# Last projection units reordered, layer norm and pooling moved between units, and the gate row summed in the middle of the kernel

## The chip, the cores and the metric

One core of a Trainium2 chip. The core has five engines that each run their own list of instructions in order: TensorE (PE in the rows; PEld is its weight load), VectorE (DVE), ScalarE (ACT), GpSimd (POOL) and SyncE (SP, which issues most transfers; GpSimd issues the rest). They meet only through semaphores: an instruction waits until a counter has reached a value. The metric is the device time of one execution in microseconds (us).

## What is computed

One mixer layer for 2,048 latent positions of width 1,024 and 256 context positions, in float32:

```python
hx = rmsnorm(x, g_pre) * (1 + sc_x) + sh_x              # sc, sh, gt = silu(c) @ w_mod + b_mod
ux = hx @ w_in                                          # 1024 -> 2304 = 18 tiles of 128
vx_lru, gx_lru, vx_pool, gx_pool, vx_conf, ggx_conf, gx_conf = split(ux)
y_lru  = bidirectional RG-LRU(dwconv4(vx_lru))          # gates by matmul, two scans, context first
y_pool = (window means - v) @ pool_w * pool_scale
y_conf = silu(layernorm(dwconv31(vx_conf * sigmoid(ggx_conf)))) @ conf_pw
z = concat(y_lru * silu(gx_lru), y_pool * silu(gx_pool), y_conf * silu(gx_conf))
out = x + gt_x * rmsnorm(z @ w_out, g_post)             # gt_x: the gate row, 1024 numbers
```

## The kernel before

Every float32 product of weight and activation is three matmuls on a high and a low half (`mm3`: hi·hi, hi·lo, lo·hi), so each operand is first split: ScalarE or GpSimd rounds the high half, VectorE or GpSimd subtracts it.

**Units.** The normalised, transposed input lies in `xTh` and `xTl` (8 blocks of 128 rows by 2,048 positions). A projection unit (o, c) computes tile o of the 18 for chunk c of 512 positions: 24 matmuls of 512 columns into one of two PSUM banks. ScalarE copies the bank into one of two slots of `ustage` (`evac`), and SP stores the slot to DRAM (`store_u`). `evac(U)` waits until the store of unit U-2 has landed; unit U waits until U-2 is evacuated. Sixteen further units (`conv`, 15 matmuls of 256 columns) are the 31-tap convolution. `UNITS` is the list of all 88, numbered 0 to 87 here; tiles are taken in the order `ORDER`, and each tile's weights are loaded into the slot of the tile two before it (`load_w`, `w_hi`, `w_lo`).

**Steps.** Beside the units runs the LRU in 20 steps q (4 channel tiles by 5 pieces). `gates(q)` are 12 matmuls that TensorE runs right behind unit `GATES_AFTER[q]`. Then ScalarE does `sigmoids(q)` and `decays(q)`, one `evac`, `roots(q)` (a square root on what VectorE's `one_minus_a2` left), and the other evacuations up to unit `GATES_AFTER[q+1]`, which come ahead of `sigmoids(q+1)` in its list. VectorE ends the step with `scans(q)`. The units behind `GATES_AFTER[5]` to `[12]` are 19, 22, 26, 29, 32, 37, 40, 43.

**SP's list.** For each unit in order: `store_u(n)`, then `after_unit(n)`, which issues what hangs on that unit: the next tile's weights and the inputs and weights of a later convolution.

**Tail.** `TAIL` is a list of tokens that every engine walks, each doing its own part of a token: `unit`; for chunk c of the layer norm `mu` (mean), `var`, `swish`, `pw` (pointwise product); for half-chunks n of the pooling `pool` (sums) and `pmm` (product); `wo` k (load and split of W_out block k); `item` n (one block of z: load y and gate, silu, multiply, split); and before also `gate` and `gmm` (gate row by 16 matmuls). Of the 20 units behind the last gates, 14 run first; the last 6 have `mu` to `pmm` of chunks 0 and 1 between them; chunks 2 and 3 follow with `wo` and `item` behind them. W_out and z lie where `xTh` and `xTl` were, so their loads begin when the last unit is done:

```python
if kind == "gate":
    sp.wait_ge(s_pu, N_CU + len(UNITS))
```

GpSimd walks the tail only behind this, which produces what the first `mu` needs (`onesk`, `la`):

```python
pool.wait_ge(s_ys, 64 * N_LRU)
pool.wait_ge(s_pu, N_CU + CONV_AT[-1] + 1)
g.memset(pwr[:], 0.0).then_inc(s_twz, 1)
g.memset(onesk[:], 1.0 / 256.0).then_inc(s_twz, 1)
```

**Stage 5.** 16 output tiles of 128 positions, 48 matmuls each; the z items of the next chunk are made meanwhile, three ahead.

Of the kernel before, what the change touches and what calls it, by code (L numbers as in the profile page):

```python
# [91 lines left out]
def mixer_kernel(nc, x, ctx, par, w_mod, b_gate, g_post, w_in, gate_w, pool_w, conv_dw, conf_pw, w_out,  # L92
# [6 lines left out]
    with es:  # L99
# [93 lines left out]
        crep = a4.take("crep", [P, KD, P])  # L193

        a5 = Area(x0, w0)
        woh = a5.take("woh", [P, KD, D], f32r)
        wol = a5.take("wol", [P, KD, D], f32r)
        z1 = a5.off
        zh = a5.take("zh", [P, 2, KD, CH], f32r)
        zl = a5.take("zl", [P, 2, KD, CH], f32r)  # L200

        zsize = 4 * KD * CH
        wg = [at("wg0", [P, KD, CH], z1 + zsize), at("wg1", [P, KD, CH], z1 + 3 * zsize)]
        ab = Area(w0, r0)
        wor = ab.take("wor", [P, 2, D])
        yb = ab.take("yb", [P, 3, CH])
        gb = ab.take("gb", [P, 3, CH])
# [153 lines left out]
        for c in range(NCH + 1):
            now, before = c < NCH, c > 0
            steps = [("mu", c) if now else None, ("swish", c - 1) if before else None,
                     ("pmm", 2 * c - 1) if before else None, rest.pop(0) if rest and now else None,
                     ("pool", 2 * c) if now else None,
                     rest.pop(0) if rest and now else None, ("var", c) if now else None, ("pw", c - 1) if before else None,
                     ("pool", 2 * c + 1) if now else None, ("pmm", 2 * c) if now else None,
                     rest.pop(0) if rest and now else None]
            for token in [token for token in steps if token]:
                TAIL.append(token)  # L370
                if ("unit", len(UNITS) - 1) in TAIL and token[0] in SIDE_BEHIND:
                    TAIL += side[:SIDE_PIECES]
                    side = side[SIDE_PIECES:]
# [12 lines left out]
        def _(sp):  # L386
# [96 lines left out]
            def load_item(n):  # L483

                c, k = ITEMS[n]
                if n >= 3:
                    sp.wait_ge(s_zl, n - 2)
                if c == 0 and k == 4:
                    sp.wait_ge(s_pys, 32)
                if c == 0 and k == 6:  # L490
                    sp.wait_ge(s_lys, 32)
# [1 line left out]
                gt = (G_LRU + k) if k < 4 else (G_POOL + k - 4) if k < 6 else (G_CONF + k - 6)
# [2 lines left out]
            def load_wg(h):
                for m in range(2):
                    sp.dma_start(wg[h][:, :, m * 256:(m + 1) * 256], w_mod[8 + 2 * h + m]).then_inc(s_wg[h], 16)

            def load_wo(k):  # L500
                if k >= 2:
                    sp.wait_ge(s_wol, k - 1)
                sp.dma_start(wor[:, k % 2, :], w_out[k * P:(k + 1) * P, :]).then_inc(s_wor[k % 2], 16)

            for kind, n in TAIL:
                if kind == "gate":
                    sp.wait_ge(s_pu, N_CU + len(UNITS))
                    sp.wait_ge(s_wlo, len(W_JOBS))
                    sp.wait_ge(s_ys, 64 * N_LRU)
                    for b in range(2):  # L510
                        sp.wait_ge(s_us[b], 16 * (N_CU + len(UNITS)) // 2)
                    load_wo(0)
                    load_item(0)
                    load_wo(1)
                    load_item(1)
                    load_item(2)
                    load_wg(0)
                if kind == "wo" and n + 2 < KD:
                    load_wo(n + 2)
# [2 lines left out]
                if kind == "item" and n == 0:
                    load_wg(1)
# [1143 lines left out]
```

## Time and profile before

| | us |
|---|---|
| median of 3 runs | 914.27 (913.06 to 915.58) |
| the profiled execution | 916.63 |
| its span, first to last instruction | 914.8 |
| TensorE busy | 788.8 |
| VectorE, ScalarE, GpSimd busy | 485.4, 455.2, 394.0 |
| mean granted TensorE clock | 0.943 |

TensorE is busy for 86% of the span. A busy TensorE is at one of two clocks, 2.4 GHz (granted clock 1.0) or 1.2 GHz, and the clock of a stretch is the mean. The idle time ahead of an instruction says more than the share: who ended it stands in brackets in the timeline.

### The profile page before, as it was taken

What the parts mean: (1) busy time and instruction counts of PE and PEld (TensorE: products, weight loads), DVE (VectorE), ACT (ScalarE), POOL (GpSimd) and SP (SyncE); (2) the same over time, 40 slices, a digit from 0 to 9 for tenths busy, and PEclk for the clock granted to TensorE, in tenths of its full rate; (3) what the DMA queues carried; (4) which work ended last, traced back from release to release, by engine and by line L of the source; (5) the groups of instructions that cost most, each with busy time, mean ns of one, the idle gap of its engine ahead of it and who ended that gap; (6) DMA issues with size and microseconds to landing.
All of it is one profiled execution on the core that took longest, in us unless ns stands there. A gap on an engine that the chain in (4) does not pass through costs nothing.

```text
span 914.8 us, 9881 instructions
## 1 busy us (share of the span) xinstructions
PE 788.8 (86%) x3496; PEld 622.0 (68%) x3496; DVE 485.4 (53%) x653; ACT 455.2 (50%) x749; POOL 394.0 (43%) x405
## 2 busy tenths in 40 slices
PE   6687998999879899899889969999547399999996
PEld 2266786888767687778677758867324287878785
DVE  4388834538744875547543300054657557475732
ACT  4265634797558856768657601114345134344311
POOL 0278444566537646555654441113303135252521
PEclk9797998999999999999999979999878799999998
DMA  9992013235332443333321332223895176657532
GB/s 366 345 275 110 35 58 104 72 86 162 109 85 73 134 146 108 103 124 109 109 84 47 115 95 70 70 92 110 237 321 157 51 276 207 219 196 233 182 116 101
DMA packets 84914, 130.10 MB, mean 142 GB/s; under 512 B 22689, under 2 KB 49953, under 8 KB 83329
## 3 DMA queue, kind: packets, MB, share of 16 engines
q1 hardware_dynamic: 80496, 115.44, 38.8%
q0 software_dynamic: 4368, 14.03, 5.6%
q8 instruction: 28, 0.46, 0.2%
q14 instruction: 22, 0.17, 0.1%
HBM read 91.17 MB, written 38.27 MB: 141 GB/s over the span
## 4 chain that ended last, share of the span: by engine, by line
PE 47%; issue 14%; ACT 13%; DVE 11%; POOL 8%; DMA 4%; SPq 3%; POOLq 0%; ACTq 0%; DVEq 0%
PE bank L1419 14%; PE bank L1421 14%; PE bank L1420 14%; SPq L392 2%; DVE zl L1365 2%; PE bank L1561 2%; ACT L928 2%; ACT Qb L929 2%; ACT Ib L916 1%; ACT bank L930 1%; DMA wraw<-in_w_in 1%; POOL zh L564 1%; DVE yb L1363 1%; DVE xTl L1157 1%; POOL Ib L658 1%
## 5 line engine op out<-in xcount | busy, mean ns | idle before, releaser
L1419 PE MATMUL bank<-xTh,wh 128*128 128x512 f32 (+1 forms) x592 | 238.2, 402 | 41.6 <-ACT ustage L903 10.6
L1421 PE MATMUL bank<-xTh,wl 128*128 128x512 f32 (+1 forms) x592 | 234.7, 396 | 0.0
L1420 PE MATMUL bank<-xTl,wh 128*128 128x512 f32 x576 | 230.4, 400 | 0.0
L1419 PEld LDWEIGHTS bank<-xTh,wh 128*128 128x128 f32 x592 | 114.9, 194 | 69.9 <-issue 35.6
L1421 PEld LDWEIGHTS bank<-xTh,wl 128*128 128x128 f32 x592 | 114.6, 194 | 24.3
L1420 PEld LDWEIGHTS bank<-xTl,wh 128*128 128x128 f32 x576 | 112.4, 195 | 23.5 <-issue 0.2
L1419 PE MATMUL bank<-woh,zh 128*128 128x512 f32 x256 | 100.0, 391 | 4.0 <-DVE zl L1365 3.2
L903 ACT ACTIVATE ustage<-bank 128x512 f32<-128x512 f32 x56 | 33.5, 600 | 135.2 <-PE bank L1421 135.1
L1420 PE MATMUL bank<-wol,zh 128*128 128x512 f32 x256 | 99.6, 389 | 0.0
L1421 PE MATMUL bank<-woh,zl 128*128 128x512 f32 x256 | 99.6, 389 | 0.0
L1086 ACT ACTIVATE sqj<-bank 128x512 f32<-128x512 f32 x32 | 18.8, 595 | 108.6 <-PE bank L1421 108.6
L687 POOL TENSOR_TENSOR wl<-wraw,wh 128x1024 fp32r<-128x1024 f32 x16 | 38.8, 2423 | 67.5 <-ACT wh L853 67.5
L564 POOL TENSOR_SCALAR sph<-xc 128x512 fp32r<-128x512 f32 (+1 forms) x36 | 23.2, 660 | 99.4 <-DVE xc L1106 51.1
L564 POOL TENSOR_SCALAR zh<-yb 128x512 fp32r<-128x512 f32 x32 | 19.9, 620 | 107.2 <-DVE yb L1363 107.2
L1419 PEld LDWEIGHTS bank<-woh,zh 128*128 128x128 f32 x256 | 48.0, 188 | 15.6 <-DVE zl L1365 4.4
L1106 DVE SCALAR_TENSOR_TENSOR bank<-Qb,bank 128x512 f32<-128x512 f32 (+1 forms) x40 | 25.4, 641 | 57.0 <-ACT bank L930 57.0
L1421 PEld LDWEIGHTS bank<-woh,zl 128*128 128x128 f32 x256 | 48.0, 188 | 10.0
L1420 PEld LDWEIGHTS bank<-wol,zh 128*128 128x128 f32 x256 | 48.1, 188 | 9.8
L1106 DVE SCALAR_TENSOR_TENSOR xc<-vbuf,prm,xc 128x512 f32<-128x512 f32 (+1 forms) x60 | 52.0, 866 | 2.1
L658 POOL TENSOR_TENSOR Ib<-Ib,xc 128x512 f32<-128x512 f32 (+1 forms) x40 | 46.9, 1194 | 1.1 <-ACT Ib L916 1.0
L564 POOL TENSOR_SCALAR xTh<-fbuf 128x512 fp32r<-128x512 f32 (+1 forms) x40 | 33.9, 867 | 31.0 <-ACT fbuf L887 30.8
L853 ACT ACTIVATE wh<-wraw 128x1024 fp32r<-128x1024 f32 x18 | 19.2, 1066 | 53.3 <-DMA wraw<-in_w_in 53.3
(190 smaller groups left out, 1536.8 us busy)
## 6 DMA issues: line engine op xcount, KB each, us to landing
scratch_u<-ustage SPq DMA_DIRECT2D x72, 256.0 KB, 2.5
wraw<-in_w_in SPq DMA_DIRECT2D x18, 512.0 KB, 4.1
wm<-in_w_mod SPq DMA_DIRECT2D x8, 1024.0 KB, 11.2
xg<-in_x SPq DMA_DIRECT2D x16, 512.0 KB, 8.8
yb<-scratch_y SPq DMA_DIRECT2D x32, 256.0 KB, 3.1
gb<-scratch_u SPq DMA_DIRECT2D x32, 256.0 KB, 4.7
xres<-in_x SPq DMA_DIRECT2D x16, 512.0 KB, 4.7
out<-tout SPq DMA_DIRECT2D x16, 512.0 KB, 2.9
```

The costliest lines, as they stand in the source:

```text
L392: sp.dma_start(rows(g, i, 0, KD), src[i * P:(i + 1) * P, :].rearrange("p (k j) -> p k j", j=P)).then_inc(s_xin[g], 16)
L564: return g.tensor_scalar(dst, src, 1.0, 1.0, ALU.mult, ALU.mult)
L658: g.tensor_tensor(out=I, in0=I, in1=xc_piece(c), op=ALU.mult).then_inc(s_ix, 1)
L687: g.tensor_tensor(out=l, in0=w_raw(w), in1=h.bitcast(f32), op=ALU.subtract).then_inc(s_wlo, 1)
L853: a.activation(W_JOBS[w][1][0], w_raw(w), ACT.Copy).then_inc(s_whi, 1)
L903: ins = a.activation(ustage[:, U % 2, :], pu[U % 2][:], ACT.Copy)
L928: a.activation(Ab[:, d, 0:n], r, ACT.Exp, scale=kn[:, kc:kc + 1]).then_inc(s_aq, 1)
L1086: a.activation(sqj[:, h * CH:(h + 1) * CH], ob[m % 3][h][:], ACT.Square, accum_out=ss2[:, h:h + 1]).then_inc(s_osq, 1)
L1106: return v.scalar_tensor_tensor(out=out, in0=in0, scalar=sc, in1=in1, op0=op0, op1=op1)
L1419: mm(out, wh_, xh_, start=first, stop=False)
L1420: mm(out, wh_, xl_, start=False, stop=False)
L1421: return mm(out, wl_, xh_, start=False, stop=last)
```

## The change

Three things are done together.

1. The last eight projections are taken in another order, so that chunks 0 and 1 of `xTh`/`xTl` are read for the last time four units before the end. W_out goes into these columns (raw and low half in the same place), z into chunks 2 and 3.
2. All of the layer norm and pooling is woven between the first 14 of the 20 units behind the last gates. Six units follow with `wo` 0 to 7 and `item` 0 to 7 behind four of them.
3. The gate row is no longer made by 16 matmuls on 4 MB of weights loaded in the tail. It is made in eight pieces of 128 columns during steps 5 to 12: SP loads piece m into `wgp` (one buffer), VectorE sums it over k in 8 instructions behind `scans(5 + m)`, and two matmuls with `onesk` behind the first output tile add up the partitions.

The first output tile also waits per block k, with both halves of the output inside the loop over k.

```diff
+PROJECTIONS = [(o, c) for c in range(NCH) for o in (0, 1)] + [(o, c) for o in range(2, NT_IN - 2) for c in range(NCH)]
+PROJECTIONS += [(16, 0), (16, 1), (17, 0), (17, 1), (16, 2), (17, 2), (16, 3), (17, 3)]
...
+GATE_STEP = [5 + m for m in range(8)]
+GATE_PIECE_AT = [GATES_AFTER[q - 1] for q in GATE_STEP]
...
-        TAIL, rest = rest[:-6], rest[-6:]
...
+        TAIL = []
         for c in range(NCH + 1):
+            now, after = c < NCH, c > 0
+            TAIL += [("mu", c)] if now else []
+            TAIL += [("swish", c - 1), ("pmm", 2 * c - 1)] if after else []
+            TAIL.append(rest.pop(0))
+            TAIL += [("pool", 2 * c)] if now else []
+            TAIL.append(rest.pop(0))
+            TAIL += [("var", c)] if now else []
+            TAIL += [("pw", c - 1)] if after else []
+            TAIL += [("pool", 2 * c + 1), ("pmm", 2 * c), rest.pop(0)] if now else []
+        HALF_DONE, THREE_DONE = PROJ_AT[-5], PROJ_AT[-3]
+        side = [("wo", k) for k in range(KD)] + [("item", k) for k in range(KD)]
+        while rest:
+            TAIL.append(rest.pop(0))
+            behind = 0 if TAIL[-1][1] < HALF_DONE else 4 if TAIL[-1][1] < THREE_DONE else 3
+            TAIL += side[:behind]
+            side = side[behind:]
         TAIL += side
...
                     if n == LAST_OF[o - 2]:
                         load_w(o + 2)
+                for m in range(KD):
+                    if n == GATE_PIECE_AT[m]:
+                        if m:
+                            sp.wait_ge(s_ga, m)
+                        sp.dma_start(wgp[:], w_mod[8 + m // 2, :, :, m % 2 * P:m % 2 * P + P]).then_inc(s_wg, 16)
...
             def load_wo(k):
-                if k >= 2:
-                    sp.wait_ge(s_wol, k - 1)
-                sp.dma_start(wor[:, k % 2, :], w_out[k * P:(k + 1) * P, :]).then_inc(s_wor[k % 2], 16)
+                if k == 0:
+                    sp.wait_ge(s_pu, N_CU + HALF_DONE + 1)
+                sp.dma_start(wo_raw(k), w_out[k * P:(k + 1) * P, :]).then_inc(s_wor[k], 16)
...
                 if kind == "unit":
                     store_u(N_CU + n)
                     after_unit(n)
+                    if n == HALF_DONE:
+                        for k in range(KD):
+                            load_wo(k)
+                        for k in range(3):
+                            load_item(k)
...
+            def gate_sum(m):
+
+                dve.wait_ge(s_wg, 16 * (m + 1))
+                acc = gacc[:, m * P:(m + 1) * P]
+                link(v.tensor_scalar(acc, wgp[:, 0, :], cs[:, 0:1], None, ALU.mult))
+                for k in range(1, KD - 1):
+                    link(stt(acc, wgp[:, k, :], cs[:, 2 * k:2 * k + 1], acc, ALU.mult, ALU.add))
+                k = KD - 1
+                stt(acc, wgp[:, k, :], cs[:, 2 * k:2 * k + 1], acc, ALU.mult, ALU.add).then_inc(s_ga, 1)
...
                 scans(q)
+                if q in GATE_STEP:
+                    gate_sum(GATE_STEP.index(q))
...
+            def gate_row():
+
+                pe.wait_ge(s_ga, KD)
+                pe.wait_ge(s_ev, N_CU + len(UNITS))
+                for h in range(2):
+                    mm(gob[h][:], onesk[:], gacc[:, h * CH:(h + 1) * CH], start=True, stop=True).then_inc(s_gmm, 1)
```

SP's list of transfers around step 5, before: the weights of a tile (`wraw`) behind unit 19, then the stores of units 20 (`scratch_u`) and 21 (`scratch_cv`, a convolution).

```order
43 L404 DMA wraw<-in_w_in 128x1024 [waits unit_done,w_lo]
44 L442 DMA scratch_u<-ustage 1024x1x64 [waits unit_evacuated]
45 L442 DMA scratch_cv<-ustage 128x256 [waits unit_evacuated]
46 L448 DMA cvwraw<-in_conv_dw 128x640 [waits unit_done]
47 L462 DMA cvz<-scratch_u 128x256 [waits u_stored0,u_stored1,unit_done]
```

The same place in the changed kernel; `gate_summed` is `s_ga`.

```order
44 L409 DMA wraw<-in_w_in 128x1024 [waits unit_done,w_lo]
45 L478 DMA wgp<-in_w_mod 128x8x128 [waits gate_summed]
46 L447 DMA scratch_u<-ustage 1024x1x64 [waits unit_evacuated]
47 L447 DMA scratch_cv<-ustage 128x256 [waits unit_evacuated]
48 L453 DMA cvwraw<-in_conv_dw 128x640 [waits unit_done]
49 L467 DMA cvz<-scratch_u 128x256 [waits u_stored0,u_stored1,unit_done]
```

The piece of gate weights, with its wait, stands between unit 19's weights and unit 20's store.

VectorE's list at the end of step 5 in the changed kernel, from the second scan on:

```order
140 L1252 SCALAR_TENSOR_TENSOR Qb<-Ab,Ib 128x256
141 L1259 COPY sml<-Qb 128x1
142 L1280 TENSOR_SCALAR gacc<-wgp,sml 128x128
143 L1105 SCALAR_TENSOR_TENSOR gacc<-wgp,sml,gacc 128x128 x7
144 L1221 TENSOR_SCALAR xc<-vbuf,prm 128x512
```

The eight instructions of the sum stand between the scan's last copy and the next piece's depthwise convolution (`xc`); before, 144 followed 141. What `gate_summed` counts is the last of them.

TensorE's list behind the last gates, before:

```order
1921 L1420 MATMUL bank<-spl,gwh 128x512
1922 L1421 MATMUL bank<-sph,gwl 128x512
1923 L1419 MATMUL bank<-xTh,wh 128x512 [waits unit_evacuated,hT_lo,w_lo]
1924 L1420 MATMUL bank<-xTl,wh 128x512
1925 L1421 MATMUL bank<-xTh,wl 128x512
```

and in the changed kernel:

```order
1921 L1426 MATMUL bank<-spl,gwh 128x512
1922 L1427 MATMUL bank<-sph,gwl 128x512
1923 L1535 MATMUL bank<-la,onesk 128x512 [waits scan_done,ln_in,tailw_zero]
1924 L1535 MATMUL bank<-la,onesk 128x512
1925 L1425 MATMUL bank<-xTh,wh 128x512 [waits unit_evacuated,hT_lo,w_lo]
```

`mu` 0 (`la`, `onesk`) now stands ahead of the units of tile 13, where it stood 14 units later.

## Rows read from the trace of the kernel before

**Rows 1.** The page: TensorE's busy time and share; GB/s moved in 40 slices.

```profile
PE 788.8 (86%) x3496; PEld 622.0 (68%) x3496; DVE 485.4 (53%) x653; ACT 455.2 (50%) x749; POOL 394.0 (43%) x405
...
GB/s 366 345 275 110 35 58 104 72 86 162 109 85 73 134 146 108 103 124 109 109 84 47 115 95 70 70 92 110 237 321 157 51 276 207 219 196 233 182 116 101
```

**Rows 2.** Busy time by stretch: length; PE, PEld, DVE, ACT, POOL; clock, DMA share, GB/s.

```profile
593.30:643.40 50.10, 46.34 (x182) 35.06 (x182) 26.04 (x34) 14.66 (x21) 10.49 (x15) 0.97 0.31 95
643.40:728.60 85.20, 43.07 (x99) 23.10 (x98) 54.30 (x68) 34.14 (x45) 21.02 (x31) 0.76 0.62 198
728.60:739.50 10.90, 10.89 (x48) 9.05 (x49) 2.58 (x4) 0.00 (x0) 0.00 (x0) 1.00 0.80 277
739.50:914.80 175.30, 164.34 (x722) 134.76 (x720) 98.66 (x129) 63.32 (x123) 59.13 (x56) 0.99 0.56 185
```

**Rows 3.** Timeline, TensorE: start, length, what, and in brackets idle time before and releaser.

```profile
506.24 0.40 PE L1421 MATMUL bank<-sph,gwl 128*128 128x512 f32 x1
...
535.99 0.80 PE L1419 MATMUL bank<-xTh,wh 128*128 128x512 f32 x1 [6.89 <-POOL wl L687]
...
593.12 0.59 PE L1529 MATMUL bank<-la,onesk 128*128 128x512 f32 x1
...
619.29 0.47 PE L1419 MATMUL bank<-pdh,pwh 128*128 128x512 f32 x1 [3.76 <-DVE pdl L1333]
...
645.85 0.47 PE L1419 MATMUL bank<-pdh,pwh 128*128 128x512 f32 x1 [0.76 <-issue]
```

**Rows 4.** Timeline, ScalarE, steps 5 to 12 (L901 evac, L853 w_hi, L912 sigmoids, L938 roots).

```profile
243.71 0.60 ACT L901 ACTIVATE ustage<-bank 128x512 f32<-128x512 f32 x1 [2.60 <-PE bank L1421]
...
265.63 0.60 ACT L901 ACTIVATE ustage<-bank 128x512 f32<-128x512 f32 x1 [4.66 <-PE bank L1421]
271.09 1.06 ACT L853 ACTIVATE wh<-wraw 128x1024 fp32r<-128x1024 f32 x1 [4.86 <-DMA wraw<-in_w_in]
...
274.58 0.66 ACT L912 ACTIVATE bank<-bank,prm 128x512 f32<-128x512 f32 x1
...
291.20 1.24 ACT L912 ACTIVATE bank<-bank,prm 128x512 f32<-128x512 f32 x2 [0.87 <-PE bank L1421]
...
300.51 1.07 ACT L938 ACTIVATE bank<-bank 128x512 f32<-128x512 f32 x2
...
368.38 1.24 ACT L912 ACTIVATE bank<-bank,prm 128x512 f32<-128x512 f32 x2 [0.88 <-PE bank L1421]
```

**Rows 5.** Timeline, VectorE: the copy that ends scans(5), and that of scans(8).

```profile
251.02 0.15 DVE L1260 COPY sml<-Qb 128x1 f32<-128x1 f32 x1
...
305.39 0.15 DVE L1260 COPY sml<-Qb 128x1 f32<-128x1 f32 x1
```

**Rows 6.** Instructions by line and shape, VectorE: count, busy us, mean ns, idle before.

```profile
L1106 DVE SCALAR_TENSOR_TENSOR bank<-Qb,bank 128x512 f32<-128x512 f32 x32 | 22.2, 695 | 55.3 <-ACT bank L930 55.3
...
L1106 DVE SCALAR_TENSOR_TENSOR bank<-Qb,bank 128x256 f32<-128x256 f32 x8 | 3.1, 423 | 1.7 <-ACT bank L930 1.7
```

**Rows 7.** DMA issues: count, KB each, median us from issue to landing.

```profile
scratch_u<-ustage SPq DMA_DIRECT2D x72, 256.0 KB, 2.5
wraw<-in_w_in SPq DMA_DIRECT2D x18, 512.0 KB, 4.1
...
gb<-scratch_u SPq DMA_DIRECT2D x32, 256.0 KB, 4.7
...
la<-scratch_cv POOLq DMA_DIRECT2D x8, 256.0 KB, 4.6
```

**Rows 8.** Timeline, GpSimd, behind the last step.

```profile
522.01 1.12 POOL L670 DMA_DIRECT2D scratch_y<-yrow  x2 [0.30 <-POOL yrow L667]
...
531.11 1.85 POOL L767 DMA_DIRECT2D la<-scratch_cv  x2
```

**Rows 9.** Timeline, VectorE, stage 5: the last instruction of two z items that follow each other.

```profile
746.89 0.69 DVE L1365 TENSOR_TENSOR zl<-yb,zh 128x512 fp32r<-128x512 f32 x1 [0.74 <-POOL zh L564]
...
748.93 0.69 DVE L1365 TENSOR_TENSOR zl<-yb,zh 128x512 fp32r<-128x512 f32 x1 [0.74 <-POOL zh L564]
```

More of the change, by code:

```diff
@@ L130, in mixer_kernel @@
         sml = fixed.take("sml", [P, 128])
+        gacc = fixed.take("gacc", [P, D])
         r0 = fixed.off
@@ L169, in mixer_kernel @@
         czl = a3.take("cvzl", [P, Z_SLOTS, NPH + 2 * REACH], f32r)
+        wgp = a3.take("wgp", [P, KD, P])
         a4 = Area(r0, end)
@@ L192, in mixer_kernel, with wo_hi, wo_lo, wo_raw @@
         onesk = a4.take("onesk", [P, P])
[L193 to L207, printed above, removed]
+        yb = a4.take("yb", [P, 3, CH])
+        gb = a4.take("gb", [P, 3, CH])
+        HALF = SEQ // 2
+        def wo_hi(k):
+            return xTh[:, k, 0:HALF]
+        def wo_lo(k):
+            return xTl[:, k, 0:HALF]
+        def wo_raw(k):
+            return xg[:, k, 0:HALF]
+        def z_cols(c):
+            return slice(HALF + c % 2 * CH, HALF + c % 2 * CH + CH)
         a6 = Area(r0, end)
@@ L278, in mixer_kernel @@
         s_pmm, s_pye, s_pys = sem("pool_product"), sem("pool_y"), sem("pool_y_stored")
-        s_wor, s_woh, s_wol = [sem(f"wo_in{b}") for b in range(2)], sem("wo_hi"), sem("wo_lo")
-        s_cr, s_gmm, s_gbc, s_gpo = sem("c_repeated"), sem("gate_product"), sem("gate_row"), sem("gpost_in")
-        s_wg = [sem(f"wgate_in{h}") for h in range(2)]
+        s_wor, s_woh, s_wol = [sem(f"wo_in{k}") for k in range(KD)], sem("wo_hi"), sem("wo_lo")
+        s_gmm, s_gpo = sem("gate_product"), sem("gpost_in")
+        s_wg, s_ga = sem("wgate_in"), sem("gate_summed")
         s_yg = [sem(f"yg_in{b}") for b in range(3)]
@@ L356, in mixer_kernel @@
         rest = [("unit", n) for n in range(GATES_AFTER[-1] + 1, len(UNITS))]
-        TAIL, rest = rest[:-6], rest[-6:]
-        side = [("gate", 0)] + [(kind, k) for k in range(KD) for kind in ("wo", "item")]
-        side[9:9], side[14:14] = [("gmm", 0)], [("gmm", 1)]
+        TAIL = []
         for c in range(NCH + 1):
[L362 to L373, printed above, removed]
+            now, after = c < NCH, c > 0
[14 more added lines that the diff above has]
+            side = side[behind:]
         TAIL += side
-        assert not rest
         ITEMS = [(c, k) for c in range(NCH) for k in range(KD)]
@@ L485, in load_item @@
                 c, k = ITEMS[n]
+                gt = (G_LRU + k) if k < 4 else (G_POOL + k - 4) if k < 6 else (G_CONF + k - 6)
                 if n >= 3:
                     sp.wait_ge(s_zl, n - 2)
+                elif n == 0:
+                    sp.wait_ge(s_ys, 64 * N_LRU)
                 if c == 0 and k == 4:
[L489 removed]
+                    sp.wait_ge(s_pys, 32 * NCH)
                 if c == 0 and k == 6:
[L491 removed]
+                    sp.wait_ge(s_lys, 32 * NCH)
+                U = unit_of(gt, c)
+                sp.wait_ge(s_us[U % 2], 16 * (U // 2 + 1))
                 sp.dma_start(yb[:, n % 3, :], y_dram[k, :, c * CH:(c + 1) * CH]).then_inc(s_yg[n % 3], 16)
[L493 removed]
                 sp.dma_start(gb[:, n % 3, :], u_dram[gt, :, c * CH:(c + 1) * CH]).then_inc(s_yg[n % 3], 16)
[L496 to L498 removed]
             def load_wo(k):
[L501 to L503 removed]
+                if k == 0:
+                    sp.wait_ge(s_pu, N_CU + HALF_DONE + 1)
+                sp.dma_start(wo_raw(k), w_out[k * P:(k + 1) * P, :]).then_inc(s_wor[k], 16)
             for kind, n in TAIL:
[L506 to L519, printed above, removed]
                 if kind == "item" and n + 3 < KD:
                     load_item(n + 3)
[L522 to L523 removed]
                 if kind == "unit":
@@ L1354, in out_weights_lo @@
                 dve.wait_ge(s_woh, k + 1)
-                v.tensor_tensor(out=wol[:, k, :], in0=wor[:, k % 2, :], in1=woh[:, k, :].bitcast(f32),
-                                op=ALU.subtract).then_inc(s_wol, 1)
+                v.tensor_tensor(out=wo_lo(k), in0=wo_raw(k), in1=wo_hi(k).bitcast(f32), op=ALU.subtract).then_inc(s_wol, 1)
             def z_item(n):
@@ L1376, in _ @@
                     ln_lo(n)
-                if kind == "gate":
-                    for b in range(2):
-                        dve.wait_ge(s_us[b], 16 * (N_CU + len(UNITS)) // 2)
-                    v.tensor_copy(crep[:], cs[:, 0:16:2].unsqueeze(2).to_broadcast([P, KD, P])).then_inc(s_cr, 1)
                 if kind == "wo":
@@ L1390, in _ @@
                 hs = slice(h * CH, (h + 1) * CH)
-                link(v.tensor_tensor(out=gbc[:, hs], in0=gbc[:, hs], in1=gob[h][:], op=ALU.add))
+                link(stt(gbc[:, hs], gob[h][:], 256.0, gbc[:, hs], ALU.mult, ALU.add))
                 link(v.tensor_tensor(out=gbc[:, hs], in0=gbc[:, hs], in1=gpo[:, hs], op=ALU.mult))
```

45 lines of the change are left out of this document (19 added, 26 removed).

## The prediction

> **What bounds the kernel now.** I read the page first, then the busy time by stretch, then TensorE's timeline for the brackets with idle time, and last the lists of ScalarE, VectorE, GpSimd and the queues around the places that the diff touches. TensorE is busy 788.8 us of 914.8 [rows 1], so it is the engine to watch, and there are two places where it waits. The large one is the stretch from 643.4, when the last unit is done, to 728.6, when the first output tile starts: 85.2 us with 43.1 busy, at a mean granted clock of 0.76, nearer to 1.2 than to 2.4 GHz, behind 0.97 ahead of it [rows 2]. The small one is in the steps. There ScalarE's list sets the pace: in step 8 it goes from the sigmoids (291.20) to the last root (301.6), and VectorE's scans end at 305.54, 14.3 us behind the sigmoids [rows 4, 5]. TensorE fits its units in between, with short pauses.
>
> I call S(q) the start of sigmoids(q) on ScalarE and E(q) the end of scans(q) on VectorE. E(5) is 251.2 and S(12) is 368.4 [rows 4, 5].
>
> **The middle: the gate row in eight pieces.** The work is small. A scalar_tensor_tensor takes 695 ns for 512 columns and 423 for 256 [rows 6]; on that line 128 columns are 0.29 us, with 0.03 to the next linked one 0.32, so a piece costs VectorE 8 x 0.32 = 2.6 us. Bounds: 8 x 0.19 = 1.5 us, if only the copy of one column (0.15 us [rows 5]) and some link were paid, and 8 x 0.51 = 4.1, somewhat over the 256-column form.
>
> The wait is not small. SP reaches piece m (m from 1) right behind the store of unit GATES_AFTER[m+4], the unit ahead of gates(m+4), and waits there for gate_sum(m-1), which VectorE does at the end of that same step m+4. SP is one list in order. Queued behind the waiting instruction are the stores of the step's units, the convolution's weights and inputs, and the next tile's weights. Call the unit n. evac(n+1) and evac(n+2) need only stores up to n. evac(n+3) needs store n+1, which is behind the wait, and it stands ahead of sigmoids(q+1) in ScalarE's list. So in each of steps 5 to 11, S(q+1) cannot come before E(q), the sum, the piece's issue, the landing of store n+1, and evac(n+3). Before, nothing tied the two so: evac(22), which is unit n+3 of step 5, ran at 243.7 [rows 4], and E(5) is 251.2.
>
> From the end of the sum to the landing of store n+1: at least 0.4 + 0.3 + 2.5 = 3.2 us if the store does not feel the piece ahead of it. A 512 KB load lands in 4.1 and a 256 KB store in 2.5 [rows 7], so 256 KB more are 1.6 and the pair would land in 5.7, if all packets went in line. I take 5.0, nearer the second, since the 512 KB go out right ahead in the same queue. Then evac 0.6 and table load 1.3: 6.9 us to S(q+1). That holds for steps 5, 10 and 11. The others have more behind the wait:
> - step 6: unit 25 is the last of its tile, so the next weights are issued only after it. From evac(25) to S(7) were 9.0 us (265.63 to 274.58, of them 4.86 for the weights [rows 4]); 5.0 + 9.0 = 14.0.
> - step 7: the convolution's weights follow the store and are rounded ahead of evac(29): 5.0 + 1.6 + 0.7 + 0.6 + 1.3 = 9.2.
> - step 8: tile weights, seventh in the queue, issued 2.7 after release, landing in some 5.5 (4.1 alone), then the 3.5 us from 271.09 to 274.58 [rows 4]: 11.7.
> - step 9 has five units: as step 7 up to evac(35) (7.9), then unit 37 (24 matmuls, 5.5) and 1.9 to the sigmoids: 15.3.
>
> Together 3 x 6.9 + 14.0 + 9.2 + 11.7 + 15.3 = 70.9. Seven sums are 18.2. S to E of steps 6 to 11: 14.3 in step 8, a little more where a convolution weight is rounded or two inputs are split; 6 x 14.8 = 88.8. S(12) is then 251.2 + 70.9 + 18.2 + 88.8 = 429.1 instead of 368.4: **+61 us**. Nothing later makes it good, because the steps behind are paced by the same list. With the low ends (sum 1.5, landing 3.2, 14.3 for S to E) it is 61 - 8 - 13 - 3 = 37; with the high ends (4.1, 5.7, and 15.5) 61 + 11 + 5 + 4 = 81.
>
> What the Trainium skill says of this place, in sentences the sum does without. Its page "DMA: Bandwidth & Descriptors", section "Anatomy of one DMA — SWDGE (gpsimd) path", states that DMA engines do not wait on semaphores and that the wait happens on the issuing sequencer ahead of dispatch; by that rule everything behind the piece is held, and it speaks against this change. The trace of before has no wait in SP's list that long ahead of stores, so it can't show it. The same section fits a transfer as 2.0 us plus bytes over 436 GB/s; the piece and the store are 0.79 MB, an estimate of 3.8 us where I take 5.0 less the store's 0.3 of issue, and the middle would be some 53 us by it.
>
> **The tail.** What starts later: `mu` 0 now stands directly behind gates(19), which end at 506.6 [rows 3]. It needs `onesk` and `la`; GpSimd makes them only after the last scratch_y transfer of 522.01 has landed, and issues `la` at 531.11, two transfers [rows 8] of 4.6 us to landing [rows 7], the second some 1 us later: 536.7. Before, the four units of tile 13 ran in that time and TensorE waited only 6.89 us, to 535.99 [rows 3]. Now all 30.1 us are idle. Then:
> - chunk 0, from `mu` 0 (593.1) to the product `pmm` 1 (619.3): 26.0 with its 3.76 us wait, and 2.4 for the first matmuls behind the pause at 1.2 GHz (12 at twice their time; behind the 6.89 us pause the first took 0.80 instead of 0.4 [rows 3]): 28.4.
> - chunks 1 to 3, each with three units: before, chunk 1 took 645.85 - 619.29 = 26.6 [rows 3]; 79.8.
> - `pmm` 7, two units, `pw` 3: 48 matmuls in a row take 10.9 us [rows 2], so a unit is 5.45: 0.7 + 10.9 + 2.7 = 14.3. Then two units, 10.9. TensorE is behind the unit that frees half of xT.
> - W_out and z. Eight blocks of 0.52 MB and three items of 0.52 MB are 5.8 MB; at 366 GB/s, the best slice [rows 1], 16 us and the latency, and the first item lands at about 17. Silu (with table) 1.9, multiply, round, subtract: first z at 20.5. An item's load waits for the subtraction three items back; z items follow each other by 2.04 us [rows 9], and a reload costs about 4 (4.7 in the rows [rows 7]). So z 4 is there at 27.3, z 7 at 34.5, z 8 at 36.5, and the tile ends at 37.9. The four last units (21.8) and the tile (10.9) alone would be 32.7: 5 us of wait. Then the gate row's two matmuls, 1.8 (it has the two-matmul form of `mu`).
>
> Sum 30.1 + 28.4 + 79.8 + 14.3 + 10.9 + 37.9 + 1.8 = 203.2. Before, from 506.6 to 739.5 [rows 2], 232.9. **-30 us.** The 16 gate matmuls and the 4 MB load, gone from the tail, are in that. Bounds: -36 if W_out and z hide wholly; -17 if every chunk has the 3.76 us wait (9) and the load runs at 277 GB/s [rows 2] (4).
>
> Stage 5 behind the first tile (175.3 [rows 2]) stays: same matmuls, same z items; the gate row's additions on VectorE moved behind the tile and cover 0.7 us more at most.
>
> **Sum.** Span 914.8 + 61 - 30 = 946. The execution of this profile took 916.63, 1.8 over its span and 2.4 above the median of the runs, so I predict 914.3 + 31 = **945 us** as the median.
>
> **Rivals.**
> - The wait is worse than said: the sums are slowed beside GpSimd, and after each pause of some 8 us TensorE restarts at 1.2 GHz, as behind the 6.89 us pause, [rows 3]. Middle +80: 965. For it: pauses grow in every step. Against: the units run beside ScalarE's list, with room. Chance 0.15.
> - On the other side: SP's wait costs little, because store n+1 is in time for evac(n+3) after all. It decides if the release comes before TensorE is done with unit n+3; then only the 30 us of the tail count, less some us: 884 to 890. For it: the piece itself is needed a whole step later. Against: in step 5 evac(22) was due 7.5 us ahead of E(5) [rows 4, 5]. Chance 0.08.
> - Both halves small: middle +37 with sums of 1.5 us and stores that pass the piece, tail -36: 915, no change. Needs four low ends. Chance 0.05.
> - The forecast, 922 to 960: 0.72.
>
> **How the numbers follow.** A measurement of this kernel tells 0.3% (2.7 us) from no change. Faster: the second rival and a part of the third, 0.09; same 0.03; slower 0.88. The range for 8 in 10 leaves the fast rival out and takes in the worse wait's centre: 920 to 966.
>
> **What would show it.** In the profile after: ScalarE's evacuation of unit n+3 released by a `scratch_u` transfer in steps 5 to 11, SP idle until VectorE's `gacc`; S(12) near 429; TensorE idle about 30 us ahead of the first `la,onesk` matmul; 26 to 27 us per chunk after it; the first output tile ending about 203 us behind the last gates, with short waits for z. Wrong would be: `wgp` issued late but stores not late, a sum of over 4 us, or chunks of 30 us and more.

## The result, and the profile of the changed kernel

The median of four runs is 951.22 us (949.6 to 951.9), beside 914.92 (913.06 to 921.94) for the kernel before: ratio 1.038, 95% interval 1.0323 to 1.0436. The change makes the kernel slower. The profiled execution has a span of 947.8 us, 33.0 more than before. That is 64.4 lost in the middle, 30.4 won between the last step's gates and the gate row behind the first output tile, and two small terms.

The page after; its second line answers to the first of [rows 1]. TensorE's busy time is nearly the same (785.1 us, before 788.8), its share falls from 86% to 83%. The last line is a part of the page's chain that ended last: the sum of the gate row (`gacc`) is now on it.

```profile
span 947.8 us, 9916 instructions
PE 785.1 (83%) x3468; PEld 624.5 (66%) x3468; DVE 496.5 (52%) x716; ACT 456.7 (48%) x749; POOL 392.8 (41%) x405
...
PE bank L1425 15%; PE bank L1426 14%; PE bank L1427 14%; DMA scratch_u<-ustage 2%; SPq L397 2%; DVE gacc L1105 2%; DMA wraw<-in_w_in 2%; ACT Ib L915 2%; ACT L927 1%; ACT Qb L928 1%; DVE Qb L1252 1%; ACT bank L929 1%; ACT bank L911 1%; DVE Ib L1242 1%; DVE xTl L1156 1%
```

**The middle.** Step 5 shows the whole mechanism. VectorE's list: the end of the scans (the copy, first of [rows 5]), then the sum in eight linked instructions, then other work.

```profile
247.85 0.15 DVE L1259 COPY sml<-Qb 128x1 f32<-128x1 f32 x1
248.04 0.29 DVE L1280 TENSOR_SCALAR gacc<-wgp,sml 128x128 f32<-128x128 f32 x1
248.37 2.68 DVE L1105 SCALAR_TENSOR_TENSOR gacc<-wgp,sml,gacc 128x128 f32<-128x128 f32 x7
250.96 0.54 DVE L1221 TENSOR_SCALAR xc<-vbuf,prm 128x512 f32<-128x512 f32 x1
```

SP's list (SPq, the issue of transfers) has a hole of 27.6 us, from the end of the issue of tile weights (222.91 + 0.60) to the piece at 251.07, right behind the sum. Behind the piece stand the stores of units that ScalarE had already evacuated. That of unit 20 could have gone at 233.1, when its evacuation ended (232.51 + 0.63 below), and went at 251.71: 18.6 us of the hole are the wait's.

```profile
222.91 0.60 SPq L409 DMA_DIRECT2D wraw<-in_w_in  x1
251.07 0.60 SPq L478 DMA_DIRECT2D wgp<-in_w_mod  x1
251.71 0.67 SPq L447 DMA_DIRECT2D scratch_u<-ustage  x1
252.43 1.56 SPq L447 DMA_DIRECT2D scratch_cv<-ustage  x1
```

ScalarE's list in the same time. The evacuation that ran at 243.71 before [rows 4] runs at 256.51, 18.57 us behind the instruction ahead of it, and what ended the wait is the transfer `scratch_u<-ustage`. The sigmoids of step 6, which start the next step, stand right behind it, after a table load.

```profile
232.51 0.63 ACT L900 ACTIVATE ustage<-bank 128x512 f32<-128x512 f32 x1
...
237.47 0.47 ACT L897 ACTIVATE ustage<-bank,prm 128x256 f32<-128x256 f32 x1
256.51 0.60 ACT L900 ACTIVATE ustage<-bank 128x512 f32<-128x512 f32 x1 [18.57 <-DMA scratch_u<-ustage]
257.12 1.28 ACT L911 ACT_TABLE_LOAD   x1
258.42 1.24 ACT L911 ACTIVATE bank<-bank,prm 128x512 f32<-128x512 f32 x2
...
432.80 1.24 ACT L911 ACTIVATE bank<-bank,prm 128x512 f32<-128x512 f32 x2
```

The last row is S(12): 432.8 instead of 368.4 [rows 4].

In the other steps the first long wait of ScalarE behind the roots ends at one of the transfers held in SP's list, but not always at the same one: at the store in steps 5 (above), 6, 10 and 11, at the convolution's weights in steps 7 and 9, at the next tile's weights in step 8.

```profile
281.82 0.60 ACT L900 ACTIVATE ustage<-bank 128x512 f32<-128x512 f32 x1 [11.91 <-DMA scratch_u<-ustage]
...
314.43 0.74 ACT L950 ACTIVATE cvwh<-cvwraw 128x640 fp32r<-128x640 f32 x1 [12.74 <-DMA cvwraw<-in_conv_dw]
...
342.95 1.06 ACT L852 ACTIVATE wh<-wraw 128x1024 fp32r<-128x1024 f32 x1 [15.10 <-DMA wraw<-in_w_in]
...
370.27 0.74 ACT L950 ACTIVATE cvwh<-cvwraw 128x640 fp32r<-128x640 f32 x1 [12.66 <-DMA cvwraw<-in_conv_dw]
...
404.84 0.60 ACT L902 ACTIVATE ustage<-bank 128x512 f32<-128x512 f32 x1 [13.16 <-DMA scratch_u<-ustage]
...
430.89 0.60 ACT L902 ACTIVATE ustage<-bank 128x512 f32<-128x512 f32 x1 [12.64 <-DMA scratch_u<-ustage]
```

Here are the middle's terms, taken from the starts and ends of each step in the timelines. "E to S" is from the end of scans(q) (its last scan, without the copy behind it) to sigmoids(q+1) for q = 5 to 11, "S to E" from sigmoids(q) to the end of scans(q) for q = 6 to 11. A negative number means that the next step began ahead of that end.

```
             S(12)-S(5)  E to S, steps 5..11                      sum   S to E
before         142.0     -4.5  6.5  1.2  4.5  9.2  -1.0  -1.0     14.9  102.5
after          209.2     10.6 17.5 12.0 15.3 20.2  10.8  11.2     97.6   87.5
short_sum      193.2      7.7 15.5  8.9 13.8 17.5   8.7   8.3     80.4   88.4
small_piece    197.0      8.6 15.9 10.2 15.0 18.9   8.6   8.5     85.7   87.2
late_issue     149.2     -4.6  5.6  1.3  5.8  7.1  -2.9  -0.2     12.1  111.6
no_pieces      144.8     -4.6  7.6  1.3  5.1 10.4   1.9   2.0     23.7   96.3
middle_only    209.5     10.5 17.9 11.8 15.3 20.0  10.9  11.1     97.5   87.4
```

**The tail.** Busy time by stretch, columns as in [rows 2]: from the last step's gates to the first matmul of `mu` 0, from there to the end of the gate row behind the first output tile, and the rest.

```profile
574.10:604.30 30.20, 0.01 (x1) 0.04 (x1) 6.78 (x8) 9.61 (x14) 12.70 (x19) 0.57 0.26 84
604.30:776.60 172.30, 160.20 (x637) 122.31 (x638) 78.73 (x100) 63.11 (x88) 42.76 (x52) 0.97 0.45 147
776.60:947.80 171.20, 163.28 (x721) 134.82 (x719) 101.63 (x132) 61.91 (x119) 59.59 (x56) 0.99 0.57 190
```

The 85.2 us at clock 0.76 with half the time idle [rows 2] are gone. In their place are 30.2 us without any matmul, at a granted clock of 0.57, and then 172.3 us with 93% busy at 0.97. TensorE's timeline, which answers to [rows 3], shows the pause, the products at the start of each chunk (632.88, 660.02, 685.00 and 710.33: 25 to 27 us from one to the next), and the waits for z in the first output tile:

```profile
573.68 0.39 PE L1427 MATMUL bank<-sph,gwl 128*128 128x512 f32 x1
604.29 1.19 PE L1535 MATMUL bank<-la,onesk 128*128 128x512 f32 x1 [30.22 <-DMA la<-scratch_cv]
...
632.88 0.70 PE L1425 MATMUL bank<-pdh,pwh 128*128 128x512 f32 x1 [3.77 <-DVE pdl L1344]
660.02 0.47 PE L1425 MATMUL bank<-pdh,pwh 128*128 128x512 f32 x1 [1.33 <-issue]
685.00 0.47 PE L1425 MATMUL bank<-pdh,pwh 128*128 128x512 f32 x1 [0.78 <-issue]
710.33 0.47 PE L1425 MATMUL bank<-pdh,pwh 128*128 128x512 f32 x1 [2.88 <-issue]
...
768.34 0.51 PE L1425 MATMUL bank<-xTh 128*128 128x512 f32 x1 [1.05 <-DVE xTl L1375]
771.23 0.50 PE L1425 MATMUL bank<-xTh 128*128 128x512 f32 x1 [1.22 <-DVE xTl L1375]
773.26 0.50 PE L1425 MATMUL bank<-xTh 128*128 128x512 f32 x1 [0.39 <-DVE xTl L1375]
774.76 1.02 PE L1570 MATMUL bank<-gacc,onesk 128*128 128x512 f32 x2
```

### The profile page after: what moved, and what is told of

It is laid out like the page before. It is cut to its first block, busy times and chain, and to the rows that moved or that the text cites. A ratio compares the mean times of both kernels' runs of the same rounds, so it can differ in the third digit from the quotient of the medians.

```text
span 947.8 us, 9916 instructions
## 1 busy us (share of the span) xinstructions
PE 785.1 (83%) x3468; PEld 624.5 (66%) x3468; DVE 496.5 (52%) x716; ACT 456.7 (48%) x749; POOL 392.8 (41%) x405
## 4 chain that ended last, share of the span: by engine, by line
PE 47%; ACT 13%; DVE 11%; issue 10%; DMA 9%; POOL 6%; SPq 4%; ACTq 0%; POOLq 0%
PE bank L1425 15%; PE bank L1426 14%; PE bank L1427 14%; DMA scratch_u<-ustage 2%; SPq L397 2%; DVE gacc L1105 2%; DMA wraw<-in_w_in 2%; ACT Ib L915 2%; ACT L927 1%; ACT Qb L928 1%; DVE Qb L1252 1%; ACT bank L929 1%; ACT bank L911 1%; DVE Ib L1242 1%; DVE xTl L1156 1%
## 5 line engine op out<-in xcount | busy, mean ns | idle before, releaser
L1425 PE MATMUL bank<-xTh,wh 128*128 128x512 f32 (+1 forms) x592 | 244.1, 412 | 76.9 <-ACT ustage L902 52.2
L1425 PE MATMUL bank<-xTh 128*128 128x512 f32 (+1 forms) x272 | 105.9, 389 | 9.2 <-DVE ewl L1131 6.5
L1427 PE MATMUL bank<-xTh,xTl 128*128 128x512 f32 x256 | 99.6, 389 | 0.0
L1426 PE MATMUL bank<-xTl,xTh 128*128 128x512 f32 x256 | 99.6, 389 | 0.0
L563 POOL TENSOR_SCALAR xTh<-yb 128x512 fp32r<-128x512 f32 x32 | 19.9, 622 | 123.1 <-DVE yb L1373 123.1
L1425 PEld LDWEIGHTS bank<-xTh 128*128 128x128 f32 x272 | 51.9, 191 | 21.1 <-DVE ewl L1131 6.7
L1426 PEld LDWEIGHTS bank<-xTl,xTh 128*128 128x128 f32 x256 | 48.1, 188 | 10.1 <-issue 0.2
L1427 PEld LDWEIGHTS bank<-xTh,xTl 128*128 128x128 f32 x256 | 48.1, 188 | 10.0
L1266 DVE TENSOR_TENSOR cvz<-cvz,cvg 128x256 f32<-128x256 f32 x16 | 15.5, 981 | 70.8 <-ACT cvg L943 70.6
L1105 DVE SCALAR_TENSOR_TENSOR xc<-vbuf,prm,xc 128x512 f32<-128x512 f32 (+1 forms) x60 | 46.6, 777 | 2.1
## 6 DMA issues: line engine op xcount, KB each, us to landing
wm<-in_w_mod SPq DMA_DIRECT2D x8, 1024.0 KB, 11.7
```

Source lines behind the costliest of these rows:

```text
L563: return g.tensor_scalar(dst, src, 1.0, 1.0, ALU.mult, ALU.mult)
L1105: return v.scalar_tensor_tensor(out=out, in0=in0, scalar=sc, in1=in1, op0=op0, op1=op1)
L1266: v.tensor_tensor(out=cz[:, j % Z_SLOTS, mid], in0=cz[:, j % Z_SLOTS, mid], in1=cg[:, j % Z_SLOTS, mid], op=ALU.mult).then_inc(s_cz, 1)
L1425: mm(out, wh_, xh_, start=first, stop=False)
L1426: mm(out, wh_, xl_, start=False, stop=False)
L1427: return mm(out, wl_, xh_, start=False, stop=last)
```

## The experiments

The theory: SP's wait for gate_sum(m-1) stands ahead of stores that ScalarE's list needs, so each step waits for the sum of the step before; the tail by itself is a gain. Rivals: the gate row's work (the sums on VectorE, the 4 MB of loads) costs the time wherever it stands, or the tail loses too. Each ratio is to the kernel before, run in turn with the experiment: its median was 918.29 us beside the first four experiments and 917.68 beside the others.

**late_issue.** The same work, with the piece of step q issued behind the first unit that follows gates(q), instead of behind the unit ahead of gates(q-1): a step and a unit later in SP's list.

```diff
-GATE_PIECE_AT = [GATES_AFTER[q - 1] for q in GATE_STEP]
+GATE_PIECE_AT = [GATES_AFTER[q] + 1 for q in GATE_STEP]
```

> The same pieces, sums and semaphore wait, but SP reaches piece m one unit behind the gates of the step that sums it, when the sum before it is done. Theory (SP's list is blocked by the wait): the stores are no longer held, S(12) falls from 432.8 to within 8 us of the 368.4 of before, median 890 to 897. Rival (the sums' work on VectorE and the extra transfers are the cost): nothing of them is gone, median stays at 945 to 951.

Measured: 891.39 us (889.84 to 897.51), ratio 0.9721 (0.9682 to 0.976). The span is 888.0, 59.8 below the changed kernel's; S(12) is 373.21, 59.6 below. So the difference is in the middle, and it is the place of a wait and not the work: the same eight loads and sums are there. In SP's list the pieces stand behind stores that are due, and no hole ends at a sum (the row x2 is two stores, the second behind the evacuation at 256.06):

```profile
234.77 0.52 SPq L447 DMA_DIRECT2D scratch_u<-ustage  x1
235.33 0.68 SPq L478 DMA_DIRECT2D wgp<-in_w_mod  x1
...
242.75 14.49 SPq L447 DMA_DIRECT2D scratch_u<-ustage  x2
257.28 0.68 SPq L478 DMA_DIRECT2D wgp<-in_w_mod  x1
```

```profile
242.74 1.28 ACT L911 ACT_TABLE_LOAD   x1
244.90 1.24 ACT L911 ACTIVATE bank<-bank,prm 128x512 f32<-128x512 f32 x2 [0.88 <-PE bank L1427]
```

The sigmoids of step 6 start at 244.90 and wait for TensorE alone, as before; in the changed kernel it was 258.42.

The sums are not as cheap here. In the changed kernel GpSimd is idle in nearly all of their time, and the seven instructions behind the first take 2.7 us (2.9 in one step). Here five of the eight sums run while GpSimd works, and take more: 6.08 us in step 7, from the rows below, and 22.2 us of VectorE in the changed kernel become 38.0 us for all eight. The three sums with GpSimd idle take 2.68, as in the changed kernel.

```profile
289.89 6.08 DVE L1105 SCALAR_TENSOR_TENSOR gacc<-wgp,sml,gacc 128x128 f32<-128x128 f32 x7
...
290.70 1.24 POOL L563 TENSOR_SCALAR sph<-xc 128x512 fp32r<-128x512 f32 x2 [5.80 <-PE bank L1427]
291.91 2.62 POOL L647 TENSOR_TENSOR spl<-xc,sph 128x512 fp32r<-128x512 f32 x2
294.48 2.65 POOL L657 TENSOR_TENSOR Ib<-Ib,xc 128x512 f32<-128x512 f32 x2
```

**no_pieces.** No loads of the gate row's weights and no sums; `gacc` is filled with zeros. It leaves out the product of the gate row.

```diff
-                        if m:
-                            sp.wait_ge(s_ga, m)
-                        sp.dma_start(wgp[:], ...).then_inc(s_wg, 16)
...
-                dve.wait_ge(s_wg, 16 * (m + 1))
-                acc = gacc[:, m * P:(m + 1) * P]
...
-                stt(acc, wgp[:, k, :], cs[:, 2 * k:2 * k + 1], acc, ALU.mult, ALU.add).then_inc(s_ga, 1)
+                v.memset(gacc[:, m * P:(m + 1) * P], 0.0).then_inc(s_ga, 1)
```

> No piece is loaded and nothing is summed; VectorE writes a zero piece instead, so the gate row lacks its product. It shows the tail's part of the change alone. Theory: S(12) 368 to 371, the tail gives 30 us and stage 5 about 4, median 880 to 888. If late_issue lies within 8 us above it, the 64 us were the wait and not the work. Rival (the tail gives less than 30, the middle costs less than 61): 900 or more.

Measured: 883.05 (881.38 to 886.86), ratio 0.9624 (0.9595 to 0.9653), S(12) 368.93, span 881.1. This is the price of the gate row's work where it does not block the stores: 888.0 - 881.1 = 6.9 us of span (the medians are 8.3 apart). Where in the kernel it is paid is not shown: S(12) is 368.93 here, and 369.06 to 373.21 in the four kernels with late pieces (late_issue and three below), whose code is the same up to there. At S(19), the last sigmoids, all four are later than the 506.58 of no_pieces, by 5.3 to 8.4 us. The rival "the work costs it wherever it stands" gets 7 of 67 us.

**short_sum.** The wait stays, the sum is its first instruction alone (seven of eight products of the gate row are left out). **small_piece.** The wait and the sum stay, pieces 1 to 7 load one eighth of their bytes (the sum reads old data for the rest).

```diff
-                link(v.tensor_scalar(acc, wgp[:, 0, :], cs[:, 0:1], None, ALU.mult))
-                for k in range(1, KD - 1):
...
+                v.tensor_scalar(acc, wgp[:, 0, :], cs[:, 0:1], None, ALU.mult).then_inc(s_ga, 1)
```

```diff
-                        sp.dma_start(wgp[:], w_mod[8 + m // 2, :, :, m % 2 * P:m % 2 * P + P]).then_inc(s_wg, 16)
+                        ks = slice(0, 1 if m else KD)
+                        sp.dma_start(wgp[:, ks], w_mod[8 + m // 2, :, ks, m % 2 * P:m % 2 * P + P]).then_inc(s_wg, 16)
```

> The wait stays where it is, the sum is one instruction of eight (the gate row is incomplete). Theory (the sum is one link of a chain that the wait closes): each of seven steps is shorter by seven instructions of 0.35 and 0.03 us, 2.6 us, in all 18: median 931 to 935. Rival (the sums' work on VectorE is the cost): nearly all is gone, 890.

> The wait and the sums stay, pieces 1 to 7 load an eighth of their bytes (64 KB; the gate row is wrong). It prices the piece ahead of the store in the queue. Theory: the store lands some 1.5 us sooner in each of seven steps: 10 us, median 939 to 943. If a store does not feel what is queued ahead, 950.

Measured: short_sum 934.33 (931.1 to 940.76), ratio 1.0185 (1.0137 to 1.0233); small_piece 941.37 (940.1 to 941.83), ratio 1.0251 (1.0226 to 1.0275). From S(5) to S(12) the first takes 16.0 us less than the changed kernel, 2.3 a step, where the seven instructions left out are 2.68; the second 12.2 less, 1.7 a step. (The profiled execution of short_sum is 6.4 over its median; the excess is behind S(12).) So both lie in the serial path that the wait makes. No run has both edits; if they add, they are 28 of the 67 us. The rest (39) is left for the link itself: the store's own latency, the evacuation, weights and units that had run beside the scans before. The piece's landing, from the view of one tile's transfers, in small_piece (where the largest is the full piece 0):

```profile
DMA to landing us min/median/max: 1.9/2.0/6.0
```

and in the changed kernel

```profile
DMA to landing us min/median/max: 4.3/4.7/5.4
```

**middle_only.** The kernel before with the pieces, the sums and the wait added, and its own tail unchanged (it computes its gate row as before, and the pieces' sum is not used). The diff is against the kernel before.

```diff
+                for m in range(KD):
+                    if n == GATE_PIECE_AT[m]:
+                        if m:
+                            sp.wait_ge(s_ga, m)
+                        sp.dma_start(wgp[:], ...).then_inc(s_wp, 16)
...
+                if q in GATE_STEP:
+                    gate_sum(GATE_STEP.index(q))
```

> The kernel before with the eight pieces and sums in its steps, at the places and with the wait of the change, and its tail as it was (the sums are not used, the gate row still comes from its 16 matmuls). Theory: the middle costs 64 us by itself and adds up with the tail: S(12) at 432 to 433, median 62 to 68 over that of the kernel before, a ratio of 1.068 to 1.075. Rival (the wait hurts only with the changed tail or with the moved areas in SBUF): under 1.03.

Measured: 986.13 (984.38 to 988.65), ratio 1.0731 (1.0694 to 1.0768). Step for step the middle is that of the changed kernel (table), S(12) is 435.11, from a start of step 5 that is 2.0 later. Spans: 984.6 - 914.8 = 69.8 for the middle alone. The tail and stage 5 alone are no_pieces: 881.1 - 914.8 = -33.7. Measured apart the two parts give +36.1, together in the changed kernel +33.0, so they add up to some 3 us. Like the change itself, this diff also sets `dynamic_dma_scratch_size` from 8192 to 4096; no run parts that from the rest, but late_issue has it too and does not lose the 60 us.

**plain_end.** On late_issue: the old order of the projections, and W_out and z loaded only behind the last unit.

```diff
-PROJECTIONS = [...] + [(o, c) for o in range(2, NT_IN - 2) for c in range(NCH)]
-PROJECTIONS += [(16, 0), (16, 1), (17, 0), (17, 1), (16, 2), (17, 2), (16, 3), (17, 3)]
+PROJECTIONS = [...] + [(o, c) for o in range(2, NT_IN) for c in range(NCH)]
...
-        HALF_DONE, THREE_DONE = PROJ_AT[-5], PROJ_AT[-3]
+        HALF_DONE = THREE_DONE = PROJ_AT[-1]
...
-            behind = 0 if TAIL[-1][1] < HALF_DONE else 4 if TAIL[-1][1] < THREE_DONE else 3
+            behind = 0 if TAIL[-1][1] < HALF_DONE else len(side)
```

> late_issue with the projections in the old order, W_out and z loaded only behind the last unit, and the layer norm and pooling still woven. It parts the tail's gain. Theory: the four units (21.8 us) no longer cover the load and split of W_out, of which 5 us were already uncovered, so the tail is 15 to 20 us longer: a median of 907 to 912. If the weave alone gave the gain: 892 to 896.

Measured: 909.53 (907.99 to 910.63), ratio 0.9894 (0.9862 to 0.9927). Its span is 20.7 over late_issue's, nearly all of it one wait ahead of the first output tile:

```profile
717.91 0.77 PE L1424 MATMUL bank<-xTh 128*128 128x512 f32 x1 [19.77 <-DVE xTl L1374]
```

So the order that frees half of xT early is worth some 20 us. The four units behind it (21.8 us) are what hides the load. (In the changed kernel `wo` and `item` stand behind five units, 83 to 87, and not four.)

**four_first.** On late_issue: four units go ahead of `mu` 0, where TensorE stood idle, twelve are woven in, and the last four have `wo` and `item` behind them as before.

```diff
-        TAIL = []
-        for c in range(NCH + 1):
+        TAIL, rest = rest[:4], rest[4:]
+        for c in range(NCH):
...
+        TAIL += [("swish", NCH - 1), ("pmm", 2 * NCH - 1)] + WO[:4] + [rest.pop(0), ("pw", NCH - 1)] + WO[4:]
+        TAIL += [rest.pop(0)] + ITEM[:3] + [rest.pop(0)] + ITEM[3:6] + [rest.pop(0)] + ITEM[6:]
```

> late_issue with the four units of tile 13 ahead of the first mean again and twelve units in the weave, so that TensorE has work while GpSimd prepares onesk and la. Theory: of the 30.2 us pause about 7 stay, and the second half of the layer norm's end overlaps the W_out load: 22 to 25 us less, median 864 to 872. Rival (the four units are missed at the end, where W_out and z then wait): under 10 us less, 882 or more.

Measured: 862.13 (861.87 to 865.74), ratio 0.9389 (0.9355 to 0.9423): 6% faster than the kernel before and 9% than the changed one, the best version of this study, and 2 us below the forecast's range. The pause ahead of `mu` 0 is 8.10 us instead of 30.56, like the 6.89 of [rows 3]:

```profile
542.37 1.19 PE L1528 MATMUL bank<-la,onesk 128*128 128x512 f32 x1 [8.10 <-issue]
```

**chunk_wait.** On late_issue: the first output tile of chunks 1 to 3 waits for all eight z blocks of its chunk at once, as the kernel before did.

```diff
-                        pe.wait_ge(s_zl, KD * c + k + 1)
+                        pe.wait_ge(s_zl, KD * c + (k if c == 0 else KD - 1) + 1)
```

> late_issue where the first tile of chunks 1 to 3 waits for all eight z blocks at once, as before. Theory (the wait per block is what shortened stage 5 from 175.3 to 171.7 us): stage 5 is 3 to 4 us longer. Rival (the order of the matmuls within a tile or the moved gate row did it): no difference, under 1 us.

Measured: 897.51 (893.73 to 898.4), ratio 0.9751 (0.971 to 0.9792), 6.1 over late_issue's median; the runs of the two overlap. In the profiled executions the stretch behind the gate row is 178.1 us instead of 171.1, twice what was forecast. The waits alone are 4.6:

```profile
753.85 0.47 PE L1425 MATMUL bank<-xTh 128*128 128x512 f32 x1 [2.76 <-DVE xTl L1375]
...
800.14 0.47 PE L1425 MATMUL bank<-xTh 128*128 128x512 f32 x1 [0.92 <-DVE xTl L1375]
...
844.86 0.47 PE L1425 MATMUL bank<-xTh 128*128 128x512 f32 x1 [0.92 <-DVE xTl L1375]
```

The other 2.4 are matmuls that take longer: TensorE is busy 165.65 us there and 163.22 in late_issue. 1.6 of them are in the chunk behind the wait of 2.76 us: its 192 matmuls take 45.36 us, those of the next chunk 43.80, and its granted clock is 0.96, where late_issue has 1.00. The rest, 0.9, is ahead of the wait, and no run parts it.

```profile
718.40:753.80 35.40, 32.69 (x144) 26.68 (x143) 27.94 (x36) 17.89 (x30) 15.74 (x16) 1.00 0.70 236
753.80:800.10 46.30, 45.36 (x192) 37.10 (x192) 28.30 (x36) 16.86 (x32) 16.30 (x17) 0.96 0.62 204
800.10:844.80 44.70, 43.80 (x192) 35.97 (x192) 27.54 (x36) 18.54 (x35) 16.31 (x17) 1.00 0.64 212
```

## Why the prediction was right, step by step

The forecast was 945 us as the median, +31 on the span; the runs gave 951.22 and +33.0.

- **SP's wait holds back store n+1, which holds back evac(n+3) and the next sigmoids.** Right for the wait: in each of steps 5 to 11 it sets the next sigmoids, and late_issue removes it and takes S(12) back by 59.6 us. The transfer at which ScalarE's long wait ends is the store in steps 5, 6, 10 and 11 only; in steps 7, 8 and 9 it is the weights queued behind it. The forecast had put them into the times of these steps, but its sign "released by a `scratch_u` transfer in steps 5 to 11" was too wide. The other-side rival (the store is in time after all, 884 to 890) needed the release to come ahead of TensorE. In step 5 TensorE's last matmul of unit 22 ended at 240.60, 10.5 us ahead of the release at 251.07:

```profile
240.21 0.39 PE L1427 MATMUL bank<-xTh,wl 128*128 128x512 f32 x1
```

- **Size of the middle**, +61 forecast, +64.4 measured (67.2 from S(5) on, because step 5 began 2.8 earlier). Sums and waits, E to S, were forecast at 70.9 + 18.2 = 89.1 and are 97.6. The sum of a piece is 3.0 us, not 2.6: the seven scalar_tensor_tensor follow each other by 0.39 instead of 0.32, since the time of one with 128 columns was drawn as a line through the forms of 512 and 256 columns. Release to landing of the store is 5.4 us in step 5 (251.07 to 256.51), not 5.0. S to E is 87.5 against 88.8. Steps 6 to 9 had the order of the forecast (14.0, 9.2, 11.7, 15.3 and the sum of 2.6; measured 17.5, 12.0, 15.3, 20.2). The longest, step 9, is 2.3 over. The rival that the sums are slowed beside GpSimd did not come true in this kernel, since GpSimd is idle beside them; in late_issue they are slowed.
- **"Nothing later makes it good"** was right in that nothing is won back. From S(12) to the end of gates(19) the kernel takes 141.3 us, before 138.2: +3.1, which the forecast put at nothing. The piece of step 12 has a sum of its own, the eighth, which the seven of the forecast did not count, and step 12 is 1.5 us longer; another 1.6 are in step 17, which has no piece. That the eighth sum is the cause is not shown: the four kernels with late pieces, with the same code there, take 139.3 to 145.0.
- **The tail**, 203.2 us forecast from the last gates to the end of the gate row, 202.5 measured: the pause 30.2 for 30.1, the rest 172.3 for 173.1. The terms cancel a little (chunks of 27.1, 25.0 and 25.3 instead of 26.6).
- **Stage 5 unchanged at 175.3**: it is 171.2. The kernel before has waits of 1.50, 0.83 and 0.83 us at the start of chunks 1 to 3, 3.2 of the 4.1 us; after the change TensorE waits for the z blocks one by one and none of those waits is left. The rest is 1.1 us less TensorE time (163.28 for 164.34). The forecast gave the waits per block no price; its 0.7 us was for the gate row's additions. chunk_wait puts the old waits back and gets +7.0, of which 4.6 is idle and 2.4 slower matmuls. The waits of before:

```profile
773.88 0.50 PE L1419 MATMUL bank<-woh,zh 128*128 128x512 f32 x1 [1.50 <-DVE zl L1365]
...
818.53 0.50 PE L1419 MATMUL bank<-woh,zh 128*128 128x512 f32 x1 [0.83 <-DVE zl L1365]
...
863.17 0.50 PE L1419 MATMUL bank<-woh,zh 128*128 128x512 f32 x1 [0.83 <-DVE zl L1365]
```

- **The sum**: 64.4 + 3.1 - 30.4 - 4.1 = 33.0. The middle is 3.7 over its forecast of 60.7, the steps behind S(12) add 3.1, stage 5 gives 4.1 back, and the tail 0.7. That only 2 us are left is partly luck: the errors cancel. Against its own median the forecast is 6 us low; 2 are in the span, the rest is that this profiled execution was 1.6 under the median of its kernel and that of before 2.4 over.
- **Small slips of the forecast's working.** A mean clock of 0.76 is 1.82 GHz, halfway between the two levels and not nearer to 1.2. Chunk 0 of before took 26.2 us and not 26.0.

The Trainium skill's page "DMA: Bandwidth & Descriptors", section "Anatomy of one DMA — SWDGE (gpsimd) path", says that a DMA's wait is made on the issuing sequencer. The rows of SP above agree: 27.6 us without an issue, and then all that was queued. Its fit, 2.0 us plus bytes over 436 GB/s, was made on transfers that GpSimd issues, and these are SP's. As an estimate it gives 2.15 for the piece of 64 KB, where small_piece has a median of 2.0, and 3.2 for 512 KB, where the changed kernel has 4.7. So here the fit is near for the small one and low for the large one. The forecast's estimate from this fit has a slip too: 5.0 less 0.3 is 4.7, 0.9 over its 3.8, and seven times 0.9 off the middle leaves some 55 us and not 53.

What stays open: whether a second buffer for the pieces, with the original place of the load, would cost less than late_issue; no run has it. Which engine passes the slower sums of late_issue on to the span, its 6.9 us over no_pieces, is not shown either. And of the 39 us of the link that neither short_sum nor small_piece touches, no run separates the store's latency from the units and weights behind it.

## What to carry to other kernels

A prefetch into a single buffer has a wait in front, and on a queue that is one list in order this wait holds everything behind it: before placing such a load, ask which stores come next in that list and who needs them. Put it where its buffer is already free when the queue gets there (here a step and a unit later: in late_issue each piece is issued 1.2 to 10.8 us after the end of the sum that frees the buffer, and one changed number is worth 60 us). When work is moved to the start of a phase, look at what its inputs wait for; four independent units in front of it took another 24 us off the span (888.0 to 863.9) and 29 off the median.
